# Weight splits further ahead around the second block's mixers, in borrowed memory

## The chip, the cores and the metric

One core of one Trainium2 chip runs the whole kernel. The metric is the device time of one execution in microseconds; the time given for a kernel is the median of its runs. Engines are called by their short names: PE (TensorE), ACT (ScalarE), DVE (VectorE), POOL (GpSimd), SP (SyncE, here only a DMA queue).

## The reference

Two transformer-like blocks of two layers each work on one sequence of 256 rows and 1024 columns, in float32. Each layer is a gated FFN, a mixer, a second gated FFN, and (first block) a gate stage or (second block) a norm. What matters here is the second block's mixer:

```python
h = rms_norm(x, mix_norm[l])
u = h @ w_in[l]                      # conv 512, pool 256, q 512, k 512, v 512 columns
y_conv = conformer_conv(u_conv, ...) # 31 taps over the rows, layer norm, silu
y_pool = multiscale_pool(u_pool, pool_w[l], pool_scale[l])
q = rms_norm(q..., q_norm[l]) * (HEAD_DIM ** -0.5)
k = rms_norm(k..., k_norm[l])
...
p = jax.nn.softmax(s, axis=-1)       # two maps a head
a = p[:, :, 0] - lam * p[:, :, 1]
...
y = jnp.concatenate([y_conv, y_pool, y_attn], axis=-1) @ w_out[l]
x = x + y
```

## The kernel before

**Units.** All weights come as 704 units of 128 x 1024 floats (512 KB), in the order in which PE uses them. An FFN takes 66 units, the first block's mixer 52, the gate stage 10, the second block's mixer 26. The second block's mixers begin at units 454 and 612 (`u0`); below, units of a mixer are counted from its first, so unit -3 is one of the last of the FFN before.

**Splits.** Each weight is used as the sum of a high and a low part. A unit passes three steps. SP loads it into one of four `raw` tiles (`sync`, L2861), as soon as DVE has made the low part of the unit four before. ACT copies it into a high tile `whi` (`split` in `scalar`, the copy is recorded at L1085), which rounds it. DVE subtracts that from `raw` into a low tile `wlo` (`split` in `vector`, L1705). There are five slots of a high and a low tile, used in turn, so ACT's copy for unit u waits until PE has used unit u - 5. PE multiplies high by high, high by low and low by high (L360 to L362 in mixers, L432 and L437 in the FFNs' first half).

**Order.** Every engine runs its own instructions in the order in which they are written, and an instruction that waits holds all behind it. In the FFN and gate stages, step k splits the unit three ahead (`step`). In the mixers the order of each engine's instructions is written out by hand, splits among them (`mixer2` in `tensor`, `scalar`, `vector`, `gpsimd`).

**The second block's mixer.** Units 0 to 3 give the convolution's input (two halves, one gates the other), 4 to 7 the queries, 8 to 11 the keys, 12 and 13 the pooled input (256 columns each, four chunks of rows a unit), 14 to 17 the values, 18 to 25 the output matrix. DVE and ACT with POOL compute one half of the channels of the 31 taps each: DVE with `scalar_tensor_tensor` (L1719), ACT with a scaled copy into one of eight tap tiles, which POOL adds (L2751). Between the taps stand the other steps:

- the sums of squares of queries and keys on DVE (L2364), their root on POOL (L2672), and the scaling out of PSUM on DVE (`head_out`);
- the high part of the pooled input on ACT (`up_high`, tile `uph`), the low part on DVE (`up_low`, tile `upl`), and pooling matmuls with both on PE (`pooled`, L927);
- the transposes of queries and keys on PE (L483) and the copies of them on ACT (`turned`), then the logits on PE (L886), which DVE adds to the slopes (`biased`, L2384), ACT exponentiates (L1525) and DVE joins to differences (`difference`, L1719), which PE transposes (`turn_maps`, L483);
- the pool groups' product on PE (L939), for which DVE scales the pooled values (`pool_mean`, L2456).

PE takes unit 14 into PSUM banks 0 and 1, which DVE must have emptied of the keys. Then come key transposes, the pooling matmuls, the logits, and unit 14's second half, unit 15 and so on. The first two jobs of unit 18 come before the transposes of the differences.

**Memory.** The mixer's work tiles are columns of one tensor `scr2` (`part2`). `pr` (4096 columns, the maps) and `aT` (2048, their transposes) are written only after the logits. `HTh` and `HTl` have eight chunks of 256 columns each, which hold the FFN's hidden values for the second matmul, and in the mixer the three parts of `y` from its second half on.

## Time and profile before

| | us |
|---|---|
| median of 3 runs | 2061.3 (2060.49 to 2064.38) |
| the profiled execution's own time | 2061.33 |
| its span, first to last instruction | 2059.5 |
| PE busy | 2041.7 |
| DVE busy | 1499.8 |
| ACT busy | 1095.3 |
| POOL busy | 128.7 |

The granted clock of PE was 0.999 over the span. The first of the two mixers in question stands at about 1309 to 1403 us of the span, the second at about 1774 to 1868. In the timelines each line gives the start in us, the duration, the engine, the line of the kernel, output and inputs by name, shapes and count. In brackets stands how long the engine was idle before it and what ended that. PE's matmuls are pipelined: one that lasts 0.39 us is followed by the next after about 0.23, so a bracket shows less than the whole time lost.

### The profile page before, as it was taken

How to read it: one execution, taken by the hardware profiler on the slowest of the kernel's cores; microseconds unless marked ns; L12 is line 12 of the kernel's file. 1: busy time of each engine (PE TensorE's matmuls, PEld its weight loads, DVE VectorE, ACT ScalarE, POOL GpSimd, SP SyncE). 2: the span in 40 equal slices, each digit the busy share in tenths (PEclk: the TensorE clock that was granted, in tenths of full speed). 3: DMA queues.
4: the chain of work that ended last, by engine and by line, in shares of the span. 5: the costliest groups of instructions: out<-in, count | busy, mean ns of one | idle time of the engine just before them, and what ended most of it. 6: DMA issues, size and time to landing. Idle time of an engine off the chain costs nothing.

```text
span 2059.5 us, 27840 instructions
## 1 busy us (share of the span) xinstructions
PE 2041.7 (99%) x10800; PEld 1742.9 (85%) x10800; DVE 1499.8 (73%) x2261; ACT 1095.3 (53%) x1637; POOL 128.7 (6%) x140
## 2 busy tenths in 40 slices
PE   9999999999999999999999999999999999999998
PEld 8888888888888888888888888878888888878887
DVE  6776677777777767677777777798667777798766
ACT  5444665544554456655446444675445544675443
POOL 1000100000000001000000000160000000160000
PEclk9999999999999999999999999999999999999999
DMA  7654545555555555455565755436565655536553
GB/s 255 200 185 162 197 153 197 185 185 186 192 189 185 188 171 174 156 198 194 184 191 186 245 184 188 171 114 202 190 193 190 199 190 184 174 113 195 194 193 124
DMA packets 105539, 378.82 MB, mean 184 GB/s; under 512 B 12173, under 2 KB 12837, under 8 KB 105152
## 3 DMA queue, kind: packets, MB, share of 16 engines
q1 hardware_dynamic: 102768, 368.95, 54.4%
q0 software_dynamic: 2208, 7.71, 1.3%
q8 instruction: 86, 1.41, 0.3%
q14 instruction: 45, 0.37, 0.1%
q10 hardware_dynamic: 432, 0.39, 0.1%
HBM read 375.73 MB, written 1.27 MB: 183 GB/s over the span
## 4 chain that ended last, share of the span: by engine, by line
PE 93%; DVE 4%; DMA 1%; ACT 1%; issue 1%; POOL 0%; POOLq 0%; DVEq 0%; ACTq 0%
PE pb L432 31%; PE pb L437 16%; PE pb L360 13%; PE pb L361 13%; PE pb L362 13%; DVE scr L1719 2%; PE pb L385 1%; DVE wlo L1705 1%; PE pb L405 1%; PE pb L407 1%; PE pb L406 1%; PE pb L483 1%; DMA raw<-in_W 1%; DVE scr L2384 0%; ACT whi L1085 0%
## 5 line engine op out<-in xcount | busy, mean ns | idle before, releaser
L1705 DVE TENSOR_TENSOR wlo<-raw,whi 128x1024 fp32r<-128x1024 f32 (+1 forms) x702 | 849.0, 1217 | 54.2 <-ACT whi L1085 53.9
L1085 ACT ACTIVATE whi<-raw 128x1024 fp32r<-128x1024 f32 (+1 forms) x706 | 730.8, 1046 | 288.7 <-PE pb L437 165.2
L432 PE MATMUL pb<-XT,whi 128*128 128x512 f32 x2816 | 703.1, 391 | 1.8 <-DVE XT L1719 1.3
L432 PEld LDWEIGHTS pb<-XT,whi 128*128 128x128 f32 x2816 | 515.5, 188 | 101.8 <-issue 1.8
L437 PEld LDWEIGHTS pb<-XT,wlo 128*128 128x128 f32 x2816 | 384.1, 190 | 27.5
L437 PE MATMUL pb<-XT,wlo 128*128 128x256 f32 x2816 | 392.6, 282 | 0.0
L1817 DVE TENSOR_REDUCE sbuf_s<-pb 128x256 f32<-128x512 f32 x240 | 154.6, 686 | 235.3 <-PE pb L437 235.3
L360 PE MATMUL pb<-whi,HTh 128*128 128x512 f32 x816 | 321.4, 394 | 0.6 <-DVE HTl L1836 0.6
L361 PE MATMUL pb<-wlo,HTh 128*128 128x512 f32 x816 | 319.4, 391 | 0.0
L362 PE MATMUL pb<-whi,HTl 128*128 128x512 f32 x816 | 317.7, 389 | 0.0
L1155 ACT ACTIVATE sbuf_s<-sbuf_s 128x256 f32<-128x256 f32 x120 | 49.7, 419 | 343.6 <-DVE sbuf_s L1824 343.6
L360 PE MATMUL pb<-whi,XT 128*128 128x512 f32 (+2 forms) x496 | 189.6, 382 | 0.9 <-DVE scr L1719 0.6
L362 PE MATMUL pb<-whi,XT 128*128 128x512 f32 (+2 forms) x496 | 186.6, 376 | 0.0
L361 PE MATMUL pb<-wlo,XT 128*128 128x512 f32 (+2 forms) x496 | 186.5, 376 | 0.0
L362 PEld LDWEIGHTS pb<-whi,HTl 128*128 128x128 f32 x816 | 153.3, 188 | 33.3
L360 PEld LDWEIGHTS pb<-whi,HTh 128*128 128x128 f32 x816 | 153.8, 189 | 28.7 <-issue 1.2
L361 PEld LDWEIGHTS pb<-wlo,HTh 128*128 128x128 f32 x816 | 153.9, 189 | 25.5
L1817 DVE TENSOR_REDUCE sums<-pb 128x256 f32<-128x512 f32 x112 | 72.2, 686 | 131.3 <-PE pb L437 131.3
L2672 POOL TENSOR_TENSOR st<-st,cst 128x2 f32<-128x2 f32 (+3 forms) x35 | 53.8, 1536 | 1720.6 <-DVE st L1730 1533.1
L360 PEld LDWEIGHTS pb<-whi,XT 128*128 128x128 f32 x496 | 93.3, 188 | 19.6 <-issue 2.3
L1155 ACT ACTIVATE sums<-sums 128x256 f32<-128x256 f32 x56 | 23.5, 419 | 159.7 <-DVE sums L1824 159.7
L362 PEld LDWEIGHTS pb<-whi,XT 128*128 128x128 f32 x496 | 93.2, 188 | 17.1
(231 smaller groups left out, 1481.8 us busy)
## 6 DMA issues: line engine op xcount, KB each, us to landing
raw<-in_W SPq DMA_DIRECT2D x694, 512.0 KB, 4.2
raw<-in_W SPq DMA_DIRECT2D x8, 264.0 KB, 2.9
scr<-in_bc POOLq DMA_DIRECT2D x2, 640.0 KB, 5.2
raw<-in_W SPq DMA_DIRECT2D x4, 256.0 KB, 4.8
scr<-scratch POOLq DMA_DIRECT2D x8, 128.0 KB, 4.2
scr<-mrow POOLq DMA_DIRECT2D x2, 512.0 KB, 5.1
scr<-in_slope POOLq DMA_DIRECT2D x1, 1024.0 KB, 11.3
scr<-in_Pg POOLq DMA_DIRECT2D x1, 1024.0 KB, 14.5
```

The lines of the kernel that those rows point to most:

```text
L360: pe.matmul(o, ah, bh, start=begin and i == 0, stop=False)
L361: pe.matmul(o, ah, bl, start=False, stop=False)
L362: ins = pe.matmul(o, al, bh, start=False, stop=end and done)
L385: ins = pe.transpose(pb[b][:, t * P:(t + 1) * P], X[:, t, c * P:(c + 1) * P], ident[:, :])
L432: pe.matmul(pb[b + j][:, :], h[:, k:k + P], xs, start=c == 0, stop=False)
L437: ins = pe.matmul(pb[b + j][:, 0:S], l[:, k:k + P], XT[:, c, 0, :], start=False, stop=c == KD - 1)
L1085: return act.activation(o, i, ACT.Copy, scale=scale)
L1155: act.activation(g, g, ACT.Silu).then_inc(*up("silu", s, f))
L1705: dve.tensor_tensor(wlo[u % W_SLOTS][:, 0:c], raw[u % RAW_SLOTS][:, 0:c], whi[u % W_SLOTS][:, 0:c].bitcast(F32), ALU.subtract).then_inc(*u ...
L1719: return dve.scalar_tensor_tensor(out=o, in0=a, scalar=s, in1=b, op0=op0, op1=op1)
L1817: dve.tensor_reduce(sums_of(f)[:, j, :], pb[b + j][:, :].rearrange("p (s t) -> p t s", s=2), AXX, ALU.add).then_inc(*up(name, s, f))
L2672: pool.tensor_tensor(r, v, cst[:, 0:1].to_broadcast([P, n]), ALU.pow).then_inc(*done)
```

## The change

`scr2` is cut in two: `pr` and `aT` move behind it into `scr3`, and six tiles `ahead0` to `ahead5` lie on the same memory. Five more slots of a high and a low tile come from this and from `HTh` and `HTl`, each lent for a range of units:

| slot | memory | from unit | to unit |
|---|---|---|---|
| aT | `aT` | -14 | 17 |
| pr0, pr1 | `pr` | -10, -6 | 13 |
| H0 | chunks 0 to 3 of `HTh`, `HTl` | 11 | 13 |
| H1 | chunks 4 to 7 | 12 | 17 |

`placed_units` gives each unit the free slot whose last user is the oldest, and ACT's copy waits for that user (`followed`). By these rules units 6 to 13 of both mixers wait for units -2, -1, 0, 1, 2, -3, -1 and 3, units 14 to 17 for 4, 5, 7 and 8, and units 18 to 22 for 13 to 17. The FFN before a mixer splits two units at its steps 48, 51 and 54, so that it is then six ahead. The orders of ACT and DVE in the mixer are written anew. Those of PE, POOL and SP are the same.

```diff
@@ -187,7 +187,8 @@
                         ("rows", 1024)])
         c2, n2 = spans([("slope", 2048), ("bc", 1280), ("wg", 256), ("cw", 64), ("z", 512), ("zp", 572),
                         ("acc", 512), ("y", 2048), ("q", 1024), ("k", 1024), ("v", 1024), ("qT", 1024), ("kT", 1024),
-                        ("pr", 4096), ("aT", 2048), ("yc", 512), ("tap", 2048)])
+                        ("yc", 512), ("tap", 2048)])
+        c3, n3 = spans([("pr", 4096), ("aT", 2048)])
         bc1, _ = spans(BC1)
         bc2, _ = spans(BC2)
         first = ExitStack()
@@ -196,6 +197,10 @@
         PTl = first.enter_context(nc.sbuf_tensor("PTl", [P, 2, S], F32R))
         first.close()
         scr2 = sb("scr2", [P, n2])
+        ahead = ExitStack()
+        ahead_w = [ahead.enter_context(nc.sbuf_tensor(f"ahead{i}", [P, UC], F32R)) for i in range(6)]
+        ahead.close()
+        scr3 = sb("scr3", [P, n3])
...
@@ -203,6 +208,8 @@
             return scr1[:, c1[name][0]:c1[name][1]]
 
         def part2(name):
+            if name in c3:
+                return scr3[:, c3[name][0]:c3[name][1]]
             return scr2[:, c2[name][0]:c2[name][1]]
...
 
+        lent = []
+        for kind, layer, n, m, u0 in stages:
+            if kind == "mixer2":
+                lent += [("aT", u0 - 14, u0 + 17, None), ("pr0", u0 - 10, u0 + 13, None), ("pr1", u0 - 6, u0 + 13, None),
+                         ("H0", u0 + 11, u0 + 13, u0 - 3), ("H1", u0 + 12, u0 + 17, u0 - 1)]
+
+        def lent_slot(name):
+
+            if name in ("pr0", "pr1", "aT"):
+                j = 2 * ("pr0", "pr1", "aT").index(name)
+                return ahead_w[j], ahead_w[j + 1]
+            c = slice(0, 4) if name == "H0" else slice(4, 8)
+            return tuple(a[:, c, :].rearrange("p c t -> p (c t)") for a in (HTh, HTl))
+
+        def placed_units():
+
+            free = {j: (-1, None) for j in range(W_SLOTS)}
+            places, followed = [], []
+            for u in range(n_units):
+                for name, first_u, last_u, behind in lent:
+                    if u == first_u:
+                        free[name] = (-1, behind)
+                    if u == last_u + 1:
+                        del free[name]
+                slot = min(free, key=lambda j: (free[j][0], str(j)))
+                before, behind = free[slot]
+                places.append(slot)
+                followed.append(before if before >= 0 else behind)
+                free[slot] = (u, None)
+            return places, followed
+
+        places, followed = placed_units()
+
+        def high_w(u):
+            return (whi[places[u]] if isinstance(places[u], int) else lent_slot(places[u])[0])
+
+        def low_w(u):
+            return (wlo[places[u]] if isinstance(places[u], int) else lent_slot(places[u])[1])
+
+        def lead(s, k):
+
+            if s + 1 < len(stages) and stages[s + 1][0] == "mixer2":
+                return AHEAD + (k >= 48) + (k >= 51) + (k >= 54)
+            return AHEAD
+
+        def split_at(s, k):
+
+            u = stages[s][4] + k
+            return range(u + (lead(s, k - 1) if k else AHEAD), u + lead(s, k) + 1)
+
...
                 w.wait_ge(*at("lo", u))
-                h, l = whi[u % W_SLOTS], wlo[u % W_SLOTS]
+                h, l = high_w(u), low_w(u)
```

In ACT's `split`, in `step`, and in ACT's order in the mixer up to the keys:

```diff
-                if u >= W_SLOTS:
-                    w.wait_ge(*at("used", u - W_SLOTS))
+                if followed[u] is not None:
+                    w.wait_ge(*at("used", followed[u]))
                 c = cols[u]
-                copy(whi[u % W_SLOTS][:, 0:c], raw[u % RAW_SLOTS][:, 0:c]).then_inc(*up("hi", u))
+                copy(high_w(u)[:, 0:c], raw[u % RAW_SLOTS][:, 0:c]).then_inc(*up("hi", u))
...
-            def step(u):
-                split(u + AHEAD)
+            def step(s, k):
+                for u in split_at(s, k):
+                    split(u)
...
-                split(u0 + 0 + AHEAD)
+                split(u0 + 6)
                 high_x(n, 4)
                 high_x(n, 6)
                 high_x(n, 5)
-                split(u0 + 2 + AHEAD)
+                split(u0 + 8)
                 high_x(n, 7)
-                split(u0 + 1 + AHEAD)
+                split(u0 + 7)
                 square_x(n, 1)
-                split(u0 + 3 + AHEAD)
-                split(u0 + 4 + AHEAD)
+                split(u0 + 9)
                 z_gate(0)
                 z_gate(1)
-                split(u0 + 5 + AHEAD)
+                split(u0 + 10)
                 conv_in(4)
                 tap(2)
                 tap(0)
                 tap(1)
+                split(u0 + 11)
                 tap(3)
-                split(u0 + 6 + AHEAD)
-                split(u0 + 7 + AHEAD)
+                split(u0 + 12)
                 tap(4)
                 tap(7)
-                split(u0 + 8 + AHEAD)
+                split(u0 + 13)
                 tap(5)
                 tap(6)
                 squares("q", 0, 7, 2)
@@ -1579,27 +1636,25 @@
                 tap(12)
                 lam_exp()
                 tap(15)
+                split(u0 + 14)
                 tap(8)
                 tap(9)
                 tap(11)
-                split(u0 + 9 + AHEAD)
+                split(u0 + 15)
                 tap(14)
-                split(u0 + 11 + AHEAD)
-                split(u0 + 10 + AHEAD)
+                split(u0 + 16)
                 tap(13)
                 squares("k", 0, 11, 0)
                 squares("k", 1, 11, 0)
-                split(u0 + 12 + AHEAD)
                 tap(16)
                 tap(10)
                 turned("q", qT2, gq, 0, 5)
-                split(u0 + 14 + AHEAD)
+                split(u0 + 18)
                 tap(17)
                 turned("q", qT2, gq, 1, 6)
-                split(u0 + 13 + AHEAD)
+                split(u0 + 17)
                 up_high(0)
                 up_high(1)
-                split(u0 + 15 + AHEAD)
                 tap(18)
```

In DVE's order, up to the differences:

```diff
                 low_x(n, 4)
-                split(u0 + 0 + AHEAD)
+                split(u0 + 6)
                 low_x(n, 5)
                 lam_mul()
                 low_x(n, 6)
-                split(u0 + 2 + AHEAD)
+                split(u0 + 8)
                 mean_x(n)
                 low_x(n, 7)
-                split(u0 + 1 + AHEAD)
-                split(u0 + 4 + AHEAD)
-                split(u0 + 3 + AHEAD)
+                split(u0 + 7)
+                split(u0 + 9)
                 z_out(1)
                 z_out(0)
                 lam_sum()
-                split(u0 + 5 + AHEAD)
+                split(u0 + 10)
                 tap(0)
                 tap(1)
                 tap(2)
+                split(u0 + 11)
                 tap(3)
                 tap(4)
+                split(u0 + 12)
                 tap(5)
                 tap(6)
+                split(u0 + 13)
                 tap(7)
-                split(u0 + 6 + AHEAD)
                 tap(8)
                 tap(9)
                 tap(10)
                 tap(11)
-                split(u0 + 7 + AHEAD)
+                split(u0 + 14)
                 head_sum("q")
                 head_mean("q")
                 tap(12)
                 tap(13)
                 tap(14)
-                split(u0 + 8 + AHEAD)
                 tap(15)
-                split(u0 + 9 + AHEAD)
+                split(u0 + 15)
                 head_out("q", q2, 0, 2)
                 head_out("q", q2, 1, 3)
-                split(u0 + 10 + AHEAD)
                 lam_sub()
                 tap(16)
                 head_sum("k")
                 head_mean("k")
                 lam_out()
                 tap(17)
-                split(u0 + 11 + AHEAD)
+                split(u0 + 16)
                 tap(18)
                 tap(19)
                 tap(20)
@@ -2544,7 +2599,7 @@
                 head_out("k", k2, 1, 1)
                 up_low(0)
                 up_low(1)
-                split(u0 + 13 + AHEAD)
+                split(u0 + 17)
                 tap(22)
                 pool_mean(0, 5)
                 biased(0, 0, 1, 2)
@@ -2558,9 +2613,8 @@
                 maps_max(0)
                 pool_mean(1, 4)
                 tap(23)
-                split(u0 + 14 + AHEAD)
+                split(u0 + 18)
                 tap(24)
-                split(u0 + 12 + AHEAD)
                 tap(25)
                 biased(1, 2, 1, 3)
                 biased(1, 3, 1, 3)
@@ -2574,7 +2628,6 @@
                 weights_ratio(0)
                 maps_max(1)
                 weights_lam(0)
-                split(u0 + 15 + AHEAD)
                 pool_low(1, 7)
```

Behind these, both engines split units 19 to 28 at the places of before.

## Rows read from the trace of the kernel before

**Rows 1.** Engine totals of the page: busy us, share of the span, instructions.

```profile
PE 2041.7 (99%) x10800; PEld 1742.9 (85%) x10800; DVE 1499.8 (73%) x2261; ACT 1095.3 (53%) x1637; POOL 128.7 (6%) x140
```

**Rows 2.** Waits of PE, whole span: waiting line, releaser, us in total, times, longest.

```profile
PE pb L483 <- DVE scr L1719: 1.6, 4, 0.6
...
PE pb L939 <- DVE scr L2456: 1.3, 2, 0.8
PE pb L886 <- DVE st L2384: 1.0, 2, 0.6
...
PE pb L360 <- DVE scr L1719: 0.6, 2, 0.3
```

**Rows 3.** Timeline of DVE in an FFN: start, duration, instruction, count, idle before, releaser.

```profile
1249.48 1.29 DVE L1817 TENSOR_REDUCE sbuf_s<-pb 128x256 f32<-128x512 f32 x2 [2.55 <-PE pb L437]
```

**Rows 4.** Timeline of ACT, first of the two mixers.

```profile
1327.61 0.90 ACT L1085 ACTIVATE scr<-scr 128x256 f32<-128x256 f32 x2
...
1350.11 1.06 ACT L1085 ACTIVATE whi<-raw 128x1024 fp32r<-128x1024 f32 x1 [1.94 <-DMA raw<-in_W]
...
1352.99 0.82 ACT L1085 ACTIVATE uph<-pb,st 128x256 fp32r<-128x256 f32 x2
```

**Rows 5.** Timeline of DVE, first mixer, the taps.

```profile
1326.70 0.41 DVE L2355 TENSOR_SCALAR scr<-scr 128x256 f32<-128x256 f32 x1 [0.74 <-ACT scr L1085]
1327.15 5.28 DVE L1719 SCALAR_TENSOR_TENSOR scr<-scr 128x256 f32<-128x256 f32 x7
...
1349.19 2.03 DVE L1719 SCALAR_TENSOR_TENSOR scr<-scr 128x256 f32<-128x256 f32 x4
```

**Rows 6.** Timeline of POOL, first mixer.

```profile
1339.28 3.08 POOL L2672 TENSOR_TENSOR st<-st,cst 128x16 f32<-128x16 f32 x1 [3.36 <-DVE st L1730]
```

**Rows 7.** Timeline of PE, first mixer, from unit 13's last matmul on.

```profile
1351.45 0.28 PE L362 MATMUL pb<-whi,XT 128*128 128x256 f32 x1
1352.03 0.47 PE L360 MATMUL pb<-whi,XT 128*128 128x512 f32 x1 [0.30 <-DVE scr L1719]
...
1354.46 0.30 PE L927 MATMUL pb<-Pg,uph 128*64 128x256 f32 x1
...
1355.79 0.49 PE L886 MATMUL pb<-scr 64*128 64x256 f32 x2 [0.21 <-ACT scr L1085]
...
1363.93 0.40 PE L360 MATMUL pb<-whi,XT 128*128 128x512 f32 x1
...
1364.93 0.50 PE L360 MATMUL pb<-whi,XT 128*128 128x512 f32 x1
...
1373.96 0.39 PE L360 MATMUL pb<-whi,HTh 128*128 128x512 f32 x1
...
1374.41 0.39 PE L362 MATMUL pb<-whi,HTl 128*128 128x512 f32 x1
1375.37 0.33 PE L483 MATMUL pb<-ident,scr 128*128 128x128 f32 x1 [0.57 <-DVE scr L1719]
...
1379.61 0.55 PE L483 MATMUL pb<-ident,scr 128*128 128x128 f32 x3 [0.23 <-DVE scr L1719]
```

**Rows 8.** Timeline of DVE, first mixer, behind the keys' normalisation.

```profile
1351.14 1.40 DVE L1719 SCALAR_TENSOR_TENSOR scr<-pb,st 128x512 f32<-128x512 f32 x2
1353.49 0.88 DVE L1719 SCALAR_TENSOR_TENSOR upl<-pb,st,uph 128x256 fp32r<-128x256 f32 x2 [0.95 <-ACT uph L1085]
...
1363.67 1.21 DVE L1705 TENSOR_TENSOR wlo<-raw,whi 128x1024 fp32r<-128x1024 f32 x1
...
1369.19 1.77 DVE L1705 TENSOR_TENSOR wlo<-raw,whi 128x1024 fp32r<-128x1024 f32 x1
```

**Rows 9.** Timeline of PE and DVE, the same places of the second mixer.

```profile
1815.92 0.28 PE L362 MATMUL pb<-whi,XT 128*128 128x256 f32 x1
...
1817.66 0.88 DVE L1719 SCALAR_TENSOR_TENSOR upl<-pb,st,uph 128x256 fp32r<-128x256 f32 x2 [0.63 <-ACT uph L1085]
...
1818.77 0.36 PE L927 MATMUL pb<-Pg,uph 128*64 128x256 f32 x1
```

More of the change, by code:

```diff
@@ L420, in gate_up @@
                         fill(b + 1)
-                    h, l = whi[u % W_SLOTS], wlo[u % W_SLOTS]
+                    h, l = high_w(u), low_w(u)
                     for i in range(4):
@@ L1164, in ffn @@
                     if u > 0:
-                        step(u)
+                        step(s, k)
                     if k == 1 and n:
@@ L1445, in gate @@
                 for k in range(10):
-                    step(u0 + k)
+                    step(s, k)
                     if k in (1, 2):
@@ L1639, in mixer2 @@
                 turned_maps(0, 0, 5)
-                split(u0 + 19 + AHEAD)
-                split(u0 + 16 + AHEAD)
-                split(u0 + 17 + AHEAD)
+                split(u0 + 22)
+                split(u0 + 19)
+                split(u0 + 20)
                 value_squares(0, 7)
@@ L1713, in split_half, with step @@
                     *(up("lo", u) if half else up("lo", u, "a")))
-            def step(u):
-                split(u + AHEAD)
+            def step(s, k):
+                for u in split_at(s, k):
+                    split(u)
             def axpy(o, a, s, b, op0, op1):
@@ L1844, in ffn @@
                     if u > 0:
-                        step(u)
+                        step(s, k)
                     if k == 1 and n:
@@ L2300, in gate @@
                 for k in range(10):
-                    step(u0 + k)
+                    step(s, k)
                     if k in (1, 2):
@@ L2602, in mixer2 @@
                 conv_norm(1, 4)
-                split(u0 + 16 + AHEAD)
+                split(u0 + 19)
                 y_sum(0)
-                split(u0 + 17 + AHEAD)
+                split(u0 + 20)
                 y_scale(0, 0)
@@ L2608, in mixer2 @@
                 y_mean(0)
-                split(u0 + 19 + AHEAD)
+                split(u0 + 22)
                 conv_low()
@@ L2616, in mixer2 @@
                 y_mean(1)
-                split(u0 + 18 + AHEAD)
+                split(u0 + 21)
                 y_root(1)
```

32 lines of the change are left out of this document (16 added, 16 removed).

## The prediction

> **What bounds the kernel now.** I read the engine totals first, then TensorE's waits, then the timelines of ACT, DVE and PE through one mixer of the second block, and last the same places of the other. PE is busy 2041.7 us of 2059.5 [rows 1]; the profiled execution took 2061.33 us, beside a median of 2061.3. So a change off PE's own work can only win back PE's waits. The four largest causes that lie in the second block's mixers are DVE results: the differences of the maps (1.6 us over four waits), the pooling (1.3), the logits' banks (1.0), and the value group's bank (0.6) [rows 2]. With the short ones that is some 2.5 us of idle PE in each of the two mixers and nothing in the FFNs that this change touches. In an FFN the DVE itself stands idle 2.55 us before each pair of sums [rows 3].
>
> By the Trainium skill (Perfetto Trace Analysis, Identifying the Most-Contended Engine) a busy share of matmuls says little of the room left, and the share of weight loads is to be read: that is 85% here [rows 1], which would leave some 315 us. All gaps of PE together are 2059.5 - 2041.7 = 17.8 us, and the sum below goes by gaps.
>
> **Units** are counted from a mixer's first (unit 0). Unit u's split is a copy on ACT (high part) and a subtraction on DVE (low part).
>
> **Lead and slots.** The FFN before a mixer now splits three units more (two at once at its steps 48, 51 and 54). Each is 1.22 us on DVE less the 0.08 by which neighbours overlap, against 2.55 us of idle time in each such group of three units [rows 3]: cost nothing. Without that cover it would be 3.4 us a mixer, but then only if PE waited. No DMA is added; loads come in the same order, each behind the subtraction four units before, so they start earlier by what the splits do. SP's queue holds nothing else. The tiles moved in memory keep their sizes: nothing.
>
> **Gate zone.** One split fewer stands before the first tap. DVE waits 0.74 us for ACT before that tap anyway, and ACT for PE's transpose: gain nothing.
>
> **From the first tap to the keys' normalisation** (1326.70 to 1352.54). Six splits before, 9 to 14; six after, 11 to 16. But four of them, not two, now come before the queries' sums, and split 11 sits behind only three taps. ACT makes its high part after tap 1: 1327.61 plus half of 0.90, plus 1.05, so 1329.1 [rows 4]; DVE is there at 1327.15 plus two pitches of 0.5, 1328.15 [rows 5]: it stands 0.95 us. Against that, seven taps there take 5.28 us beside POOL's additions and four later ones 2.03 [rows 5], a stretch of 0.25 each, and some of the taps now fall clear of the additions. The root for the queries takes POOL 3.08 us [rows 6]; its cover on DVE shrinks from two splits to one. Call d the lateness of the keys' normalisation. Lower end -0.5 (a few taps unstretched, the first wait covered). Upper end +3.2 (the 0.95 plus two splits of 1.14 in front of the root, nothing given back). After split 15, DVE still has only one split less before the key sums, which wait for PE's unit 11 as before, so I take d = 0, nearest to the unchanged total of six splits.
>
> By the Trainium skill (SBUF — State Buffer, SBUF: two separate sides) a DVE operation with two SBUF inputs and a GpSimd operation that reads SBUF exclude each other for a whole instruction. The one split seen beside additions took 1.77 us, not 1.22 [rows 8]: 0.55 more. For splits 11 to 13 that is 1.65 us by the row, and by the rule up to one addition of about 0.8 each, 2.4.
>
> **Split 18, the step that costs.** It is put on ACT ahead of tap 17, the second turned query, split 17 and the two high parts of the pooled input. Its slot is the one that unit 13 used: once the lent slots are handed back, slot choice by age gives unit 18 the slot of unit 13 in both mixers, so ACT's whole queue waits for the last matmul of unit 13. That starts at 1351.45 and lasts 0.28 [rows 7], so the wait ends at 1351.75. Behind it come split, tap, turned query, split, two high parts. The same six pieces in the same order of sizes took from 1350.11 to 1352.99 + 0.82, 3.70 us [rows 4]. New end of the high parts: 1355.45, instead of 1353.81. DVE's two low parts ended 0.56 after them (1353.49 + 0.88) [rows 8]: now 1356.01. The pooling matmuls on PE, which need them, start at 1356.10 instead of 1354.46 [rows 7]: +1.64. The following 0.21 us of waiting for the turned keys goes [rows 7], since ACT makes the first of those a tap and a copy behind the high parts, about 1356.5, and PE ends the pooling at 1357.2: +1.43 at the logits. DVE's split 17, tap 22 and the first means shift by the same 1.64 less 0.16, +1.48; the waits of PE on the logits' banks and the pooling stay, as both sides shift. PE's wait of 0.30 for the value group's bank, which follows the keys, is absorbed: unit 14 starts at 1352.03 and the pooling 2.43 later, some 0.15 of it a wait for the low parts [rows 7], so the keys may be late by d = 1.8 before they, and not ACT, set the pooling's start.
>
> **What is given back.** Unit 15's low part came last, at 1363.67 + 1.21 [rows 8]; it is now old. From 1363.93 to 1364.93 PE issued three matmuls whose pitch is (1374.41 - 1373.96)/2 = 0.225 [rows 7]: 0.32 us back. PE then stands +1.16. On DVE two splits leave the stretch before the differences, 15 (1.14 net) and 18 (1.69 net) [rows 8]; with the 1.48 that is -1.35, so the difference for which PE was held until 1375.37 is there at 1374.0. PE, free at 1374.41 + 0.23, arrives at 1375.8. That wait, 0.73 us, goes: +0.43. The later wait of 0.23 [rows 7] hangs on exponentials which wait for value evictions behind PE's unit 17; between 0 and 0.23 back, I take 0.1: **+0.3 in the first mixer**.
>
> **Second mixer.** Unit 13 ends at 1815.92 + 0.28 = 1816.20 [rows 9]. Plus 3.70, 0.56 and 0.09 gives 1820.55 for the pooling, against 1818.77: +1.78. Here no 0.21 wait stood there to be absorbed beyond 0.04, and DVE's low parts go from 1817.66 + 0.88 to 1820.46, +1.92 [rows 9], which carries the logits' banks: +1.9. Less 0.32, 0.73 and 0.1: **+0.8**.
>
> Sum: 2061.33 + 0.3 + 0.8 = 2062.4. What decides is that a stall of 1.6 to 1.9 us is made at unit 18 and 1.15 us of old stalls fall away behind it.
>
> **Rivals.**
> 1. *The stall isn't there, the relief is* (faster). If the wait of split 18 ended earlier, or its followers' lateness were covered, only 0.32 + 0.73 + 0.1 would be left, 1.15 a mixer: 2059.0. With the value group's wait (0.30 of idle, 0.46 with the refill) gone as well: 2058.1. For it: every wait it removes is in the rows. Against: PE holds unit 13 until 1351.75 while ACT was at that place at 1348.2, and the low parts had no slack to PE (0.09).
> 2. *The keys come late* (slower). The mechanism is one: the two additional splits before the queries' sums delay POOL's root, then the queries, then the keys. With d = 3.2, PE reaches the pooling 3.2 late and not 1.64 or 1.78: 1.5 more in each mixer, 2065.4. It decides from d = 1.8. For it: the 0.95 us stand at split 11 and the splits beside additions. Against: PE's unit 11 holds the key sums until 1346 anyway, and the number of splits up to the keys is unchanged. On the skill's 2.4 us for splits 11 to 13, d would pass 1.8 by 0.6 and give some 2063.6; with the row's 1.65 it stays under it.
> 3. *It moves nothing.* ACT stood 1.94 us for a load just before [rows 4]; if that wait was longer than I think the new one replaces it, and stall and relief cancel: 2061.3.
>
> **Chances and numbers.** Forecast 0.57, rival 1 0.20, rival 2 0.10, rival 3 0.13. Time 2062.4. The likeliest case by itself spans 2061.2 to 2063.8 (no 0.1s, or DVE's shift 0.4 larger in each). The range takes both rivals in: from 2058.3 to 2065.6. A difference under 0.2%, 4.1 us, is what a measurement of this kernel can't tell from none. Beyond it below (2057.2) four fifths of the 5.0 us that PE idles in both mixers would have to go: 0.04. Beyond it above (2065.4) rival 2 at its full price or worse: 0.08. Within: 0.88.
>
> **What the profile of the changed kernel would show.** ACT idle about 3.5 us before a weight copy until 1351.8, released by PE, in both mixers (right), or no such gap (rival 1). The low parts on DVE starting 1.6 us later, with DVE idle some 2 us or more before them. PE with a gap of 1.5 us at the pooling matmuls, none at unit 15 and none at the first turned differences. If the gap on PE is at the value group instead and over 1.8 us, rival 2. DVE busy more in the last third of the FFNs before, with no gap on PE there; a gap there would be a step that I priced at nothing. The forecast is wrong if the mixers' end moves by more than 2 us either way.

## The result and the profile after

| | before | after |
|---|---|---|
| median of 6 runs each, same chip | 2060.91 (2060.46 to 2064.38) | 2067.24 (2066.03 to 2070.86) |
| the profiled execution's own time | 2061.33 | 2070.58 |
| its span | 2059.5 | 2068.7 |
| PE busy | 2041.7 | 2048.5 |

The ratio is 1.0032, interval [1.0022, 1.0043]: slower by 6.3 us, where 1.1 was forecast and the range ended at 2065.6. The six executions fall in two groups by the granted clock of PE over the span: 2066.03, 2066.34 and 2066.65 at 0.999 or 1.0, and 2067.83, 2070.58 and 2070.86 at 0.997. The profiled one is of the second group, and the text says below which part of its time is the clock's. The first group too lies above the range.

Totals of the page, after, beside [rows 1]. PE has 6.8 us more of busy time with the same 10800 matmuls; DVE and ACT have no more than before.

```profile
PE 2048.5 (99%) x10800; PEld 1747.0 (84%) x10800; DVE 1499.7 (72%) x2261; ACT 1093.9 (53%) x1637; POOL 128.4 (6%) x140
```

Waits of PE, whole span, after (line <- releaser: us in total, times, longest), beside [rows 2]. L984 is the pooling (before L927), L417 the first of a unit's three products (before L360), L943 the logits, L540 the transposes.

```profile
PE pb L984 <- DVE upl L1775: 3.7, 2, 1.9
PE pb L417 <- DVE scr L1775: 1.7, 2, 0.8
...
PE pb L943 <- DVE st L2440: 1.2, 2, 0.9
PE pb L996 <- DVE scr L2512: 1.2, 2, 0.7
...
PE pb L540 <- DVE scr L1775: 0.6, 3, 0.2
```

The first row is the forecast stall. The second has the form of the old wait for the value group (0.6, L360) but is another, at another place. The transposes' 1.6 us fell to 0.6, as forecast.

**The stall.** ACT in the first mixer, then DVE (start, duration, instruction, idle before, releaser), beside [rows 4] and [rows 8]:

```profile
1353.61 1.06 ACT L1142 ACTIVATE whi<-raw 128x1024 fp32r<-128x1024 f32 x1 [4.11 <-PE pb L419]
...
1356.49 0.82 ACT L1142 ACTIVATE uph<-pb,st 128x256 fp32r<-128x256 f32 x2
```

```profile
1356.98 0.88 DVE L1775 SCALAR_TENSOR_TENSOR upl<-pb,st,uph 128x256 fp32r<-128x256 f32 x2 [2.86 <-ACT uph L1142]
```

ACT stands 4.11 us before split 18, until PE has used unit 13. The six pieces from there to the high parts then take 1356.49 + 0.82 - 1353.61 = 3.70 us (3.70 forecast), and PE stands before the pooling, in the first mixer and then in the second:

```profile
1357.96 0.30 PE L984 MATMUL pb<-Pg,uph 128*64 128x256 f32 x1 [1.85 <-DVE upl L1775]
...
1828.17 0.30 PE L984 MATMUL pb<-Pg,uph 128*64 128x256 f32 x1 [1.86 <-DVE upl L1775]
```

**What the prediction had not seen: the queries' banks.** PE, POOL and DVE, first mixer, after:

```profile
1346.66 0.36 PE L417 MATMUL pb<-HTh,XT 128*128 128x256 f32 x1 [0.83 <-DVE scr L1775]
```

```profile
1342.66 3.07 POOL L2725 TENSOR_TENSOR st<-st,cst 128x16 f32<-128x16 f32 x1 [6.12 <-DVE st L1786]
```

```profile
1329.48 1.79 DVE L1760 TENSOR_TENSOR HTl<-raw,HTh 128x1024 fp32r<-128x1024 f32 x1 [0.93 <-ACT HTh L1142]
...
1335.86 1.76 DVE L1760 TENSOR_TENSOR wlo<-raw,whi 128x1024 fp32r<-128x1024 f32 x1
...
1341.15 1.21 DVE L2420 TENSOR_REDUCE st<-sbuf_h 128x16 f32<-128x1024 f32 x1
...
1345.77 1.41 DVE L1775 SCALAR_TENSOR_TENSOR scr<-pb,st 128x512 f32<-128x512 f32 x2
...
1352.71 1.41 DVE L1775 SCALAR_TENSOR_TENSOR scr<-pb,st 128x512 f32<-128x512 f32 x2
```

The same steps before, on DVE and PE:

```profile
1337.78 1.21 DVE L2364 TENSOR_REDUCE st<-sbuf_h 128x16 f32<-128x1024 f32 x1
...
1343.21 1.40 DVE L1719 SCALAR_TENSOR_TENSOR scr<-pb,st 128x512 f32<-128x512 f32 x2
...
1344.96 0.28 PE L360 MATMUL pb<-whi,XT 128*128 128x256 f32 x1
```

Unit 12 goes into banks 2 and 3, which hold the queries until DVE has scaled them out (1345.77). Before, that step began at 1343.21 and unit 12 at 1344.96 without a wait. DVE's square sums moved from 1337.78 to 1341.15, POOL's root from 1339.28 to 1342.66 (its 3.08 us are in [rows 6]) and the scaling 2.56 later. The keys, behind it in DVE's order, are scaled 1.57 later: 1352.71 against 1351.14 [rows 8].

**The clock.** Windows of PE in the first mixer (columns: us, busy us and instructions of PE, PEld, DVE, ACT and POOL, granted clock, DMA share, GB/s):

```profile
1358.00:1365.00 7.00, 5.37 (x42) 4.10 (x44) 6.87 (x22) 4.03 (x11) 6.19 (x8) 1.00 0.23 78
1365.00:1372.00 7.00, 7.00 (x24) 4.38 (x23) 6.53 (x25) 5.72 (x21) 4.33 (x5) 0.52 0.22 75
```

and in the second:

```profile
1829.00:1833.00 4.00, 4.00 (x21) 2.81 (x20) 3.20 (x10) 2.45 (x7) 3.49 (x5) 0.57 0.38 131
```

In the first mixer, behind PE's gaps at the pooling (1.85 us), the logits (0.95) and the pool groups (0.68), the granted clock is 0.5, or 1.2 GHz, from 1364.93 on for 6.83 us. In the second it is 0.5 from 1829.15 on for 3.41 us, 1 us behind the end of the gap at the pooling (1.86) and before the gaps at the logits and the pool groups. Matmuls of 512 columns start 0.43 us apart at this half clock and not 0.227. The trace of before has no such stretch in its mixers. The Trainium skill (TensorE: Matmul & The Clock Gate, A second HAM failure mode: psum-queue depth-cycling) says that frequent short idles of PE let the clock go back and forth; these rows agree with the direction of it.

**Matmuls from the borrowed (lent) tiles.** PE by line and form, first mixer, 1312 to 1345:

```profile
L419 PE MATMUL pb<-whi,XT 128*128 128x512 f32 x23 | 9.0, 391 | 0.0
L418 PE MATMUL pb<-wlo,XT 128*128 128x512 f32 x23 | 9.0, 389 | 0.0
...
L419 PE MATMUL pb<-ahead,XT 128*128 128x512 f32 x20 | 7.9, 395 | 0.0
L418 PE MATMUL pb<-ahead,XT 128*128 128x512 f32 x20 | 7.9, 395 | 0.0
```

Those that read `ahead` last 395 ns and start 0.2335 us apart on the mean; those that read `whi` or `wlo` last 389 and start 0.2267 apart.

**The sum.** I subtracted the start of each of the 10800 matmuls before from the same one after. Where the difference jumps, PE lost (or, with a minus, won back) that many us:

| | first mixer | second mixer |
|---|---|---|
| slow matmuls, FFN end included | +0.7 | +0.7 |
| queries' banks (unit 12) | +1.07 | +1.07 |
| value group's bank | -0.20 | -0.22 |
| pooling | +1.92 | +2.11 |
| keys' copies | -0.28 | -0.08 |
| logits' banks, pool groups | +0.39 | -0.45 |
| half clock | +3.0 | +1.5 |
| unit 15's low part | -0.1 | -0.4 |
| differences | -0.79 | -0.78 |
| the rest, up to the next FFN | +0.1 | -0.0 |
| at the end of the mixer | +5.8 | +9.2 (3.4 more) |

Without the 4.5 us of half clock 4.7 are left, 2066.0. In the second mixer the waits at the logits and the pool groups, the -0.45, stand behind the slow stretch and are shorter for it; counted against it, the half clock costs some 4.1 in all, which leaves 5.1, or 2066.4. The three executions of the first group lie at 2066.0 to 2066.7. The table is a sum in PE's order of time: a delay that ends in a wait for DVE would have been a longer wait without it, so its rows aren't what each cause would cost by itself.

### The profile page after: what moved, and what is told of

Same layout as the page of the kernel before. It is cut to its first block, busy times and chain, and to the rows that moved or that the text cites. A ratio compares the mean times of both kernels' runs of the same rounds, so it can differ in the third digit from the quotient of the medians.

```text
span 2068.7 us, 27830 instructions
## 1 busy us (share of the span) xinstructions
PE 2048.5 (99%) x10800; PEld 1747.0 (84%) x10800; DVE 1499.7 (72%) x2261; ACT 1093.9 (53%) x1637; POOL 128.4 (6%) x140
## 4 chain that ended last, share of the span: by engine, by line
PE 95%; DVE 3%; ACT 1%; POOL 1%; issue 0%; DMA 0%; POOLq 0%; DVEq 0%; ACTq 0%
PE pb L489 31%; PE pb L494 16%; PE pb L417 13%; PE pb L418 13%; PE pb L419 13%; PE pb L442 1%; PE pb L540 1%; PE pb L464 1%; PE pb L462 1%; PE pb L463 1%; DVE scr L1775 1%; POOL st L2725 1%; DVE wlo L1760 1%; ACT whi L1142 0%; ACT scr L1142 0%
## 5 line engine op out<-in xcount | busy, mean ns | idle before, releaser
L1142 ACT ACTIVATE whi<-raw 128x1024 fp32r<-128x1024 f32 (+1 forms) x682 | 705.5, 1045 | 286.7 <-PE pb L494 156.9
L1760 DVE TENSOR_TENSOR wlo<-raw,whi 128x1024 fp32r<-128x1024 f32 (+1 forms) x678 | 819.9, 1217 | 50.2 <-ACT whi L1142 49.8
L489 PE MATMUL pb<-XT,whi 128*128 128x512 f32 x2784 | 695.2, 391 | 1.4 <-DVE XT L1775 1.3
L489 PEld LDWEIGHTS pb<-XT,whi 128*128 128x128 f32 x2784 | 509.7, 188 | 100.3 <-issue 1.8
L417 PE MATMUL pb<-whi,HTh 128*128 128x512 f32 x800 | 315.0, 394 | 0.0
L418 PE MATMUL pb<-wlo,HTh 128*128 128x512 f32 x800 | 313.1, 391 | 0.0
L419 PE MATMUL pb<-whi,HTl 128*128 128x512 f32 x800 | 311.5, 389 | 0.0
L417 PEld LDWEIGHTS pb<-whi,HTh 128*128 128x128 f32 x800 | 150.8, 189 | 27.1 <-DVE wlo L1760 0.2
L417 PE MATMUL pb<-whi,XT 128*128 128x512 f32 (+2 forms) x432 | 166.9, 386 | 0.2
L419 PE MATMUL pb<-whi,XT 128*128 128x512 f32 (+2 forms) x432 | 163.9, 379 | 0.0
L418 PE MATMUL pb<-wlo,XT 128*128 128x512 f32 (+2 forms) x432 | 163.7, 379 | 0.0
L417 PEld LDWEIGHTS pb<-whi,XT 128*128 128x128 f32 x432 | 81.6, 189 | 16.7 <-issue 2.2
L419 PEld LDWEIGHTS pb<-whi,XT 128*128 128x128 f32 x432 | 81.5, 189 | 15.5
```

The source lines that it names most:

```text
L417: pe.matmul(o, ah, bh, start=begin and i == 0, stop=False)
L418: pe.matmul(o, ah, bl, start=False, stop=False)
L419: ins = pe.matmul(o, al, bh, start=False, stop=end and done)
L489: pe.matmul(pb[b + j][:, :], h[:, k:k + P], xs, start=c == 0, stop=False)
L1142: return act.activation(o, i, ACT.Copy, scale=scale)
L1760: dve.tensor_tensor(low_w(u)[:, 0:c], raw[u % RAW_SLOTS][:, 0:c], high_w(u)[:, 0:c].bitcast(F32), ALU.subtract).then_inc(*up("lo", u))
```

## Experiments

Theory A: in each mixer the new place of ACT's split 18 costs a stall of 1.9 us, the queries' banks 1.1 by the new order of DVE, the borrowed tiles 0.6 by slower matmuls; the half clock is an effect of PE's gaps. Rivals stand with each run. Times are medians of 11 runs (fill16 6, align 5, high 2) in groups that share the runs of before. The before of each group is 2061.78 (late18, late18_q, fill16, align), 2061.59 (q_alone, before_stall, place, fill3), 2060.86 (pair, high) and 2061.78 (match, match256). The groups ran on different chips and their medians of before differ by 0.9 us, so times of different groups are compared through their own before. All runs but fill16 and fill3 have the same instructions, in another order or place. The granted clock of an execution is a mean over its span; it can't tell for sure whether there is a stretch of 3.4 us at half clock (the profiled execution of before_stall has one, at a mean of 0.999), so where only the mean is known, the text says so.

### late18

```diff
-                split(u0 + 18)
                 tap(17)
                 turned("q", qT2, gq, 1, 6)
                 split(u0 + 17)
                 up_high(0)
                 up_high(1)
+                split(u0 + 18)
```

> The changed kernel, with ACT's split of unit 18 behind the two high parts of the pooled input instead of three steps ahead of them. Theory A (ACT held at unit 18 makes the stall at the pooling matmuls, and the stall makes the clock fall): PE's gap of 1.85 us at the pooling goes, no stretch at the lower clock is left, and what stays are the wait for the queries' banks (1.07 us a mixer) and slower matmuls from the lent tiles (0.6 a mixer), less the 1.15 a mixer that unit 15 and the differences give back: 2061 to 2062.5. Rival B (the three splits more in the FFN or the denser taps are the cost): over 2065, with the stall moved elsewhere.

2061.78 (2060.93 to 2063.78), ratio 1.0 [0.9991, 1.0009], as A says; rival B (over 2065) falls. PE's wait at the pooling is gone, its trace has no stretch of half clock in the mixers, all runs are at 0.999. Against the changed kernel at full clock (2066.0 to 2066.7) one line carries some 4.5 us (5.4 when each is set against its own before), 4.0 of them the two pooling jumps. At the ends of the two mixers PE is 0.53 and 0.78 us behind the kernel before, where 5.8 and 9.2 stood.

### late18_q

late18, and DVE's splits at the places of before up to the keys, ACT's split 16 behind the key squares:

```diff
 tap(0); tap(1); tap(2)
-split(u0 + 11)
 tap(3); tap(4)
-split(u0 + 12)
 tap(5); tap(6)
-split(u0 + 13)
 tap(7)
+split(u0 + 11)
 tap(8); tap(9); tap(10); tap(11)
-split(u0 + 14)
+split(u0 + 12)
 head_sum("q"); head_mean("q")
 tap(12); tap(13); tap(14)
+split(u0 + 13)
 tap(15)
-split(u0 + 15)
+split(u0 + 14)
 head_out("q", q2, 0, 2); head_out("q", q2, 1, 3)
+split(u0 + 15)
```

> As late18, and in addition DVE's splits up to the keys at the places that splits had in the kernel before (two, not four, ahead of the queries' sums), ACT's split of unit 16 behind the key squares. Theory A: the wait of PE for the queries' banks goes too (1.07 us a mixer), so 2.1 us less than late18: 2059 to 2060.5, under the kernel before. Rival F (the queries are late for another reason, as POOL's root or the additions): less than 0.5 us below late18.

2058.99 (2058.8 to 2060.1), ratio 0.9984 [0.9975, 0.9993]: 2.8 below late18 and 2.8 below before, where A said 2.1 below late18. Rival F (less than 0.5) falls, and the wait for the queries' banks is gone. What is left of PE's waits on DVE in these mixers is

```profile
PE pb L996 <- DVE scr L2512: 1.6, 2, 0.9
...
PE pb L943 <- DVE st L2440: 1.0, 2, 0.6
```

The lent slots are worth something once the two orders are out of the way: units 14 and 15 are early (0.4), the differences are not waited for (0.8).

### q_alone

The second half of late18_q without the first: DVE as in before up to the keys, split 18 early.

> The changed kernel with DVE's splits up to the keys at the places they had before, and ACT's split 16 behind the key squares; ACT's split 18 stays where the change put it. Theory A (the change costs two separate things in each mixer: a wait of PE for the queries' banks, about 1.3 us, and the stall of split 18, about 1.9 us, behind which the clock can fall): the wait at the second half of the key units goes, the gap of 1.85 us before the pooling matmuls stays; against the changed kernel at full clock (about 2066.2) that is 2063.5, and up to 4.4 more in executions whose granted clock falls. Rival B (the two are one: without the late queries ACT and DVE also reach the pooled input earlier): gap at the pooling under 1 us, 2060.5 to 2062. On the clock: if it is the sum of PE's gaps in this stretch that lets it fall, it stays at 0.999 or more in all executions once the gap of 0.8 us ahead is gone; if it is the stall at the pooling itself, some executions still show 0.996 to 0.998.

2064.97 (2064.13 to 2066.33), ratio 1.0015 [1.0006, 1.0024]. The queries' wait is gone, the stall is not (1.93 us on PE, ACT idle 3.66):

```profile
1356.56 0.30 PE L984 MATMUL pb<-Pg,uph 128*64 128x256 f32 x1 [1.93 <-DVE upl L1775]
```

So the two costs are separate, as A says, and rival B falls. A's 2063.5 for full clock was missed: the four executions at 0.999 took 2064.95 to 2065.15, like the median. Part of it is the group (its before is 2061.59, the changed kernel's was 2060.91): against their own before, the changed kernel's first group lost about 5.4 and these four 3.4, so 2.0 came back where 2.7 was forecast. Seven of the 11 executions show a clock of 0.997 or 0.998; the profiled one has half clock for 3.41 us in the second mixer, 1.5 us behind the pooling's gap and before any other gap there. Its first mixer has gaps of 1.93, 0.88 and 0.69 and keeps the clock. Removing the gap at the queries' banks was not enough to keep it everywhere.

### before_stall

The kernel before, one line of ACT moved:

```diff
                 split(u0 + 14 + AHEAD)
+                split(u0 + 15 + AHEAD)
                 tap(17)
                 turned("q", qT2, gq, 1, 6)
                 split(u0 + 13 + AHEAD)
                 up_high(0)
                 up_high(1)
-                split(u0 + 15 + AHEAD)
```

> The kernel before with one line of ACT moved: its split of unit 18 (which waits for PE's last use of unit 13) goes from behind the two high parts of the pooled input to ahead of tap 17. No slot, no lead and no other order is changed. Theory A: the stall is made by this place alone. ACT idle until unit 13's last matmul, the pooling matmuls of PE 1.6 to 1.9 us later in each mixer, and nothing given back, because splits 15 and 18 of DVE still stand ahead of the differences: 2061.3 + 3.3 to 3.8 = 2064.6 to 2065.1 at full clock, up to 4.4 more in executions where the granted clock falls to half for a few us behind it. Rival B (the stall hurts only together with the other new orders): within 1 us of before, 2061 to 2062.3.

2065.09 (2064.46 to 2067.39), ratio 1.0018 [1.0009, 1.0027]: +3.5, inside A's 3.3 to 3.8, and rival B falls: this place of split 18 makes a stall without any other part of the change. But it is not the stall of the changed kernel, and the sum behind A's range did not hold. ACT, first mixer, then PE's waits at the pooling in both:

```profile
1353.10 1.06 ACT L1085 ACTIVATE whi<-raw 128x1024 fp32r<-128x1024 f32 x1 [1.43 <-DMA raw<-in_W]
```

```profile
1357.45 0.30 PE L927 MATMUL pb<-Pg,uph 128*64 128x256 f32 x1 [2.29 <-DVE upl L1719]
...
1823.56 0.34 PE L927 MATMUL pb<-Pg,uph 128*64 128x256 f32 x1 [2.45 <-DVE upl L1719]
```

What ACT waits for last is the load of unit 18, which follows the subtraction of unit 14, and not PE's use of unit 13. So the pooling comes later than in the changed kernel: by 2.4 and 2.7 us against before, where 1.9 and 2.1 stood. And something is given back, where A had nothing: the wait before the differences goes here too (0.7 and 0.8). The profiled execution ends 3.9 us behind before in its two mixers, with half clock for 3.42 us in the second, 0.1 us behind the gap of 2.45. That the median fell in A's range is in part luck. That PE's unit 13 ends the wait in the changed kernel is shown by that kernel's own row (4.11, released by PE) and, for the price, by late18.

### fill16 and fill3

Filler matmuls of 256 columns on PE, whose results are overwritten. fill16 has only the first group:

```diff
+fill(5); 16 x pe.matmul(pb[5][:, 0:256], XTh[:, 0, 0:P], XTh[:, 0, :], start=True, stop=True)
 pooled(0, 5)
 ...
+fill(4); 8 x the same into pb[4]
 pooled(1, 4)
 logits(1, 0, (5, 6))
+fill(7); 6 x the same into pb[7]
 pool_groups(7)
```

> The changed kernel, with 16 additional 256-column matmuls (about 1.9 us) on PE in the gap before the first pooling, their result overwritten. Theory A (the clock falls because PE idles there): the gap is filled at no cost, the granted clock stays at its upper level through both mixers, and the time is that of the changed kernel's undisturbed runs, 2066 to 2066.5, with no run above 2067. Rival C (the clock falls for another reason, or the fillers only add to the path): stretches at half clock stay, or the time rises by up to 3.8 us.

2068.35 (2065.74 to 2071.24), three of six runs at 0.997 or 0.998. Theory A said full clock in all: it failed in this form. Its trace has half clock for 6.83 us in the second mixer, behind gaps of 0.94 and 0.69 us that the fillers had left; the first mixer has gaps of 0.95 and 0.67 at the same places and no half clock.

> The changed kernel with filler matmuls of 256 columns, whose results are overwritten, in all three gaps of PE around the logits: 16 before the first pooling matmuls, 8 before the second, 6 before the pool groups' product. The engine stays busy where it stood 1.85, 0.95 and 0.70 us. Theory A2 (idle PE in this stretch as a whole lets the clock fall; filling the first gap alone was not enough): granted clock 0.999 or more in all executions, 2066.0 to 2066.8, no stretch of matmuls at double spacing. Rival C (the clock falls for something other than idle PE there): some executions still at 0.996 to 0.998, up to 2071.

2066.74 in a narrow band (2066.15 to 2067.13), all 11 at 0.999 or 1.0, no stretch of half clock in the mixers of its trace:

```profile
1358.00:1365.00 7.00, 7.00 (x57) 5.38 (x55) 6.87 (x23) 3.96 (x14) 6.19 (x8) 1.00 0.25 78
1365.00:1372.00 7.00, 7.00 (x37) 5.42 (x34) 6.96 (x26) 6.05 (x21) 3.90 (x5) 1.00 0.21 75
```

The band ends where the changed kernel's bad executions begin (2067.83). So idle time of PE in this stretch is what lets the clock fall, and no single gap is needed: the pooling's gap alone stood ahead of the slow stretch in the second mixers of the changed kernel, q_alone and before_stall, and only the two others in fill16. The same gaps at other times left the clock as it was; what decides between the two is not shown. The fillers buy back the clock and nothing of the stall.

### align, place, pair, high: why are matmuls from the lent tiles slow?

```diff
 align:   scr2 gets 24 unused columns, so that the lent tiles begin at byte 191488 and not 191392
 place:   ahead and scr3 are allocated before scr2, at byte 131488 (on late18_q)
 pair:    pr0 = ahead0, ahead2; pr1 = ahead1, ahead3 (on late18_q)
 high:    before.py with raw, whi, wlo, HTh, HTl allocated behind XT, X and the small tiles
```

> The changed kernel, with 96 bytes of padding before the lent tiles, so that they start at a multiple of 128 bytes instead of an odd multiple of 32; pr, aT and what follows move with them. Theory D (matmuls read weights at an unaligned address some 7 ns slower each): units in the lent tiles return to a pitch of 227 ns, 0.6 us less a mixer, 1.2 in all: 2066.0 against 2067.2. Rival E (they are slower because ACT and DVE write next to them, or by their place in memory): pitch and time unchanged within 0.4 us.

2070.17 (2069.07 to 2071.28); spacing still 0.233, so theory D falls. All five executions are at 0.997 or 0.998, and the trace has the same two stretches of half clock as the changed kernel's, so the time can't be set against that kernel's median. A 128-byte boundary is not it.

> The version with the late split 18 and the old DVE order for the queries (2059.0), with the lent tiles and scr3 allocated before scr2, some 60 KB lower in each partition; nothing else changed. Theory P (matmuls whose moving operand lies in the lent tiles are slow, 0.233 us apart instead of 0.227, because of where these lie in memory): they come down to 0.227, 0.5 us less in each mixer, 2058.0. Rival R (it is not the address but what the other engines do while they are read, or that two tiles far apart are read in turn): the spacing stays at 0.233, time 2059.0 within 0.3.

2059.37 (2058.62 to 2061.64), against 2058.0 by theory P; spacing still 0.233 with the tiles 60 KB lower. The address by itself is not it, up to here.

> The version with the late split 18 and the old DVE order for the queries (2059.0), with the lent tiles paired otherwise: slot pr0 takes ahead0 and ahead2, pr1 takes ahead1 and ahead3, 8 KB from high to low part; aT keeps ahead4 and ahead5, 4 KB apart, as a control. Theory D (matmuls that read their moving operand in turn from two tiles exactly 4 KB apart come 0.233 us apart; the slots whi/wlo are 20 KB apart and HTh/HTl 8 KB, and show 0.227): the units in pr0 and pr1 come down to 0.227, those in aT stay at 0.233, some 0.3 us less a mixer, 2058.4. Rival U (the high region of memory, above 128 KB in a partition, whatever the pairs): all stay at 0.233, 2059.0 to 2059.4.

2059.63 (2058.63 to 2060.91), all lent units at 0.233, those 8 KB apart like those 4 KB apart. The distance from high to low part is not it.

> The kernel before with raw, the five slots of split weights, HTh and HTl allocated behind the smaller tiles and XT and X, some 40 KB higher in each partition; order, sizes and distances are the same. Theory U2 (matmuls slow down to 0.233 us by the address of their moving operand, from some point between 90 and 128 KB): the slots that fall above it slow down all through the kernel; with all of them it would be 3% of some 1900 us, about 2115, with HTh and HTl alone 1 us or more. Rival D (distances or order, not addresses): 2061.3 within 0.5, spacing 0.227 in the mixers as before.

2076.03 (two executions, 2075.77 and 2076.28), ratio 1.0073 [1.0054, 1.0091]. Neither theory had this time, and the trace says more than the time. First `high`, first mixer and an FFN before it, then the same FFN in the kernel before:

```profile
L362 PE MATMUL pb<-whi,XT 128*128 128x512 f32 x39 | 15.4, 395 | 0.0
L361 PE MATMUL pb<-wlo,XT 128*128 128x512 f32 x39 | 15.4, 395 | 0.0
...
L432 PE MATMUL pb<-XT,whi 128*128 128x512 f32 x35 | 9.0, 395 | 0.0
...
L362 PE MATMUL pb<-whi,HTl 128*128 128x512 f32 x11 | 4.3, 390 | 0.0
```

```profile
L432 PE MATMUL pb<-XT,whi 128*128 128x512 f32 x38 | 9.5, 390 | 0.0
```

Everything that pairs `XT` with the weights is slow now, whichever of the two is the moving one; weights with `HTh`, moved by the same amount, are not. In `high` `whi` begins at byte 74144 and `XT` at 16512; before, they were at 32896 and 90240, and `HTh` at 73856. The pairs that are fast lie a whole number of KB apart, the slow ones do not.

### match and match256

late18_q with 56 or 120 unused columns at the end of `scr2`: the lent tiles at 191616 or 191872, which is 99 KB or 99.25 KB above `XT`.

```diff
-                        ("yc", 512), ("tap", 2048)])
+                        ("yc", 512), ("tap", 2048), ("align", 56)])
```

> The version with the late split 18 and the old DVE order for the queries (2059.0), with 56 unused columns (224 bytes) at the end of scr2. The lent tiles then begin at byte 191616 of a partition, XT at 90240: a whole number of KB apart, as whi, wlo, HTh and HTl are from XT. Theory M (two matmul operands are read at 0.227 us a matmul when their places in a partition are congruent, by some power of two, and at 0.233 when not: in the runs so far the slow pairs were ahead at 191392, 191488 and 131488 against XT at 90240, and whi at 74144 against XT at 16512, while whi against HTh, moved together, stayed fast): the lent units come down to 0.227 in both mixers, 0.5 us each, 2058.0. Rival V (something else of XT's place or of the tiles): they stay at 0.233, 2059.0 to 2059.6.

> As the run with 56 columns, with 120 (480 bytes): the lent tiles begin at 191872, a multiple of 256 bytes but not of 512 from XT. Under theory M this tells the modulus: 0.227 and 2058.0 if 256 bytes are enough (128 were not: 191488 was slow), 0.233 and 2059.0 if it takes 512 or more. Rival V: 0.233 in both kernels.

Both bring the spacing of the lent units to 0.2267 us. By form, first mixer, late18_q and then match:

```profile
L419 PE MATMUL pb<-ahead,XT 128*128 128x512 f32 x20 | 7.9, 395 | 0.0
L418 PE MATMUL pb<-ahead,XT 128*128 128x512 f32 x20 | 7.9, 395 | 0.0
```

```profile
L419 PE MATMUL pb<-ahead,XT 128*128 128x512 f32 x20 | 7.8, 389 | 0.0
L418 PE MATMUL pb<-ahead,XT 128*128 128x512 f32 x20 | 7.8, 389 | 0.0
```

Rival V falls. A difference that is a multiple of 256 bytes is enough; with align it was 101248 bytes, a multiple of 128 only, and slow. The times, 2058.70 (2057.70 to 2060.03), ratio 0.9985 [0.9976, 0.9993], and 2059.16 (2058.03 to 2061.51), ratio 0.9985 [0.9976, 0.9994], can't be told from late18_q's 0.9984; what the spacing gives back is read from the traces. From 1250 to the end of the first mixer PE gains 1.30 us on before in match and 0.86 in late18_q, in the second mixer 1.33 and 0.92: 0.44 and 0.41 more, some 0.9 in all, where theory M had 1.0. Up to unit 11 of the first mixer the slow matmuls cost late18_q 0.76 us, but 0.28 of it came back at the value group's bank, for which PE then had not to wait. match is the lowest median of all kernels run, 2058.7.

## Why the prediction was wrong

**Lead, slots, gate zone: nothing.** Right, but for one thing no term stood for: the tiles' place. "The tiles moved in memory keep their sizes: nothing" was wrong. The matmuls that read them lose 0.7 us a mixer, 1.4 in all, of which 0.9 reach the end where nothing else stands in the way (match against late18_q). In the changed kernel PE comes to the queries' banks later by this and waits there for DVE all the same, so there the net price was not isolated.

**From the first tap to the keys: d = 0. This is the step that failed.** The keys' normalisation was not on time: it began 1.57 us later (1351.14 to 1352.71), of which PE brought less than 0.2 into the mixer, so d was about 1.4, and 1.4 again in the second mixer. The reason given, that the key sums wait for PE's unit 11 as before, did not hold: they ran at 1347.82 and not 1346.25, behind the late scaling of the queries. Below 1.8 this d did not decide the pooling, as the prediction says, and PE even found the value group's bank 0.20 us sooner relative to itself, but only because it had been stopped before. The keys were also the wrong deadline. The step looked at who waits for the keys and not at who waits for the queries, whose banks PE needs 7 us sooner, and the sum has no term for them. Its own working had the ingredients, "the 0.95 plus two splits of 1.14 in front of the root": the 0.95 came true as 0.93 and the sums moved by 3.37. The scaling came 2.56 later, and PE, itself 0.6 later by the slow matmuls, lost 1.07 a mixer on it, 2.1 in all (late18_q, q_alone: gone). Rival 2 had this mechanism with the wrong victim: it asked for the keys to be late by more than 1.8, and they were by 1.4.

**Splits beside the additions.** The row of 1.77 us held: 1.79 and 1.76 for splits 11 and 13, 1.21 for 12. The Trainium skill's rule (SBUF — State Buffer, SBUF: two separate sides) would have made it up to 0.8 for each; the runs show 0.57, 0.54 and 0. The sums of the queries were late by more than this: the wait of 0.93 and two splits more in front of them are in the 3.37.

**Split 18.** The mechanism and the place were right, and the size nearly: +1.92 and +2.11 where +1.64 and +1.78 stood. The stall is fixed to the end of unit 13, so the 0.20 that PE gained at the value group's bank in between only lengthened the wait; the other 0.08 is ACT's start. The logits' 0.39 in the first mixer was taken as 0. late18 takes the stall away by one line; before_stall makes one at the same place in the old kernel, though there a load ends the wait.

**What is given back.** Right: 0.73 forecast and 0.79 measured for the differences, 0.32 and 0.4 for unit 15 (in late18 and in the second mixer; in the first the half clock hides it). The later wait of 0.23 stayed, where 0.1 was taken.

**The sum.** It also had no term for a stall on PE that costs more than its length. In the profiled execution 4.1 to 4.5 us of 9.2 are the half clock, and the median of six, 2067.24, has some 1 us of it. The gaps of 1.85, 0.95 and 0.68 in seven microseconds were all forecast in kind; that the clock answers to them was not. Without this the time would still have been above the range.

At full clock: 1.1 forecast, 4.7 measured (5.1 with the clock's net price). The difference of 3.6 is, in PE's order of time, 2.1 for the queries' banks, 1.4 for the slow matmuls, 0.6 for the pooling, less 0.4 of the value group's bank and small terms. Rival 3, that the new wait replaces an old one, did not come: the 1.94 us that ACT stood for a load [rows 4] are within the 4.11. Rival 1 (faster, 2059.0 or 2058.1, so 2.3 or 3.2 below before) is near what the change gives without its two orders: late18_q shows 2.8 below its before.

## What to carry to other kernels

When splits move ahead of a statistic, list every bank that the later step frees and the time at which the bounding engine wants each, not only the last one in the chain. On an engine that runs its instructions in order, a wait belongs behind the work that others need, even when its operation is wanted soon. A gap of one or two microseconds on PE is to be priced above its length, for the clock may fall behind it. And a tile that moves in memory with its size unchanged can still change the pace of the matmuls that read it: compare their spacing.

## What was not expected of the hardware

- Two operands of a matmul of 512 columns in 4-byte floats give 0.2267 us a matmul when their places in a partition differ by a multiple of 256 bytes (16384, 40960, 57344, 101376 and 101632 in these runs), and 0.2335 when not (differences of 101152, 101248, 41248 and 57632 bytes, all of them 32 or 128 above a multiple of 256; other remainders weren't run). The last through the whole kernel cost 15 us (`high`, two executions). It does not matter which of the two is the moving one. Why the hardware does this is not shown.
- After a pause or a run of transposes the first two to ten matmuls of fast pairs come about 0.232 apart (0.224 to 0.236, the very first 0.31 to 0.34), and then 0.227.
- Half clock for 3.4 or 6.8 us came behind gaps of PE that were each under 2.5 us, three times behind a single one (1.86, 1.94 and 2.45) with no other in the 4 us ahead of it. By the mean clock (0.997 or 0.998) it touched 3 of 6 executions of the changed kernel, 7 of 11 of q_alone and none of 11 with the three gaps filled (fill3). Without the stall at split 18 it is rarer but not absent: none of 22 in late18 and late18_q, 6 of 44 at 0.998 in place, pair, match and match256, and 5 of 33 executions of the kernel before, beside q_alone, at 0.997 or 0.998, which took 2063.9 to 2065.3. Whether each of these had a stretch at half clock in a mixer is known only for the profiled ones. It is a matter of likelihood.
